# The 32 sample rows as four concurrent fp32 tiles, and the order of loads and products around two output blocks, in a decoder step on one core

## The reference

```python
def even_layer(...):                     # ends in
    out = concat([o_a, y]) @ W["w_out_even"][e]          # (rows, 512 + 1024) @ (1536, 1024)
def odd_layer(h, o_idx, W, past):
    proj = h @ W["w_in_odd"][o_idx]                      # h: rows x 1024
    q, k, v, glr, r = _split(proj, [512, 512, 1024, 16, 1024])
    lg = log_sigmoid(glr @ W["gla_w_gate2"][o_idx] + W["gla_b_gate"][o_idx]) / GLA_TAU
    ...
    return o @ W["w_out_odd"][o_idx], st                 # (rows, 1024) @ (1024, 1024)
def apply_layer(x, c, pos, l, W, past):
    shift, scale, gate = split(silu(c) @ W["w_mod"][l] + W["b_mod"][l])
    h = rms_norm(x, W["norm_w"][l]) * (1 + scale) + shift
    out, st = ...
    return x + gate * out, st
```

## Time and profile before

| | |
|---|---|
| median of three executions | 1732.21 us |
| the profiled execution | 1730.93 us, span 1729.3 us, mean granted clock 0.97 |
| TensorE busy | 1593.2 us, 92% of the span |
| weight loads / VectorE / ScalarE / GpSimd busy | 1273.3 / 794.7 / 611.5 / 379.5 us |
| DMA | 129.90 MB, mean 75 GB/s |
| even output block | 1003 to 1180 us |
| GLA projection | from 1180.5 us, value products to about 1299 us |
| odd output block | 1610 to 1729 us |

### The profile page before, as it was taken

The page is one execution under the profiler, slowest core; times in us unless marked ns, Lnnn a source line. Parts: engine busy times, 40 slices in busy tenths (PEclk is TensorE's granted clock), DMA queues, the critical chain, the costliest instruction groups (busy, mean ns, idle before and its releaser), DMA issues. The chain is left out here.

```text
span 1729.3 us, 27074 instructions
## 1 busy us (share of the span) xinstructions
PE 1593.2 (92%) x11401; PEld 1273.3 (74%) x11401; DVE 794.7 (46%) x1283; ACT 611.5 (35%) x1144; POOL 379.5 (22%) x244
## 2 busy tenths in 40 slices
PE   4899899999999899999999869998999999998698
PEld 4589676666666799999887648876999955554485
DVE  3443202666666676610588544224313344445443
ACT  4334211655555532321265433325322302222221
POOL 1142000101100132321598632111121200000231
PEclk9999999999999999999999979998999999997799
DMA  9322543421111011111011382102101120003621
GB/s 330 104 85 49 127 98 117 126 99 50 50 50 50 5 50 49 37 49 41 13 37 38 91 244 73 49 40 80 50 1 37 39 97 0 25 25 111 222 101 63
DMA packets 119678, 129.90 MB, mean 75 GB/s; under 512 B 16728, under 2 KB 91914, under 8 KB 119430
## 3 DMA queue, kind: packets, MB, share of 16 engines
q1 hardware_dynamic: 118950, 127.56, 23.6%
q0 software_dynamic: 608, 0.63, 0.3%
HBM read 107.05 MB, written 23.18 MB: 75 GB/s over the span
## 5 line engine op out<-in xcount | busy, mean ns | idle before, releaser
L154 PE MATMUL banks<-h_T_rest,w_ssd_high 128*128 128x352 f32 x480 | 156.3, 326 | 0.0
L154 PE MATMUL banks<-h_T_high,w_ssd_high 128*128 128x352 f32 x480 | 156.1, 325 | 0.0
L154 PE MATMUL banks<-h_T_high,w_ssd_rest 128*128 128x352 f32 x480 | 155.5, 324 | 0.0
L154 PE MATMUL banks<-w_r,h_T 128*128 128x512 f32 (+1 forms) x320 | 116.4, 551 | 0.0
L1403 DVE TENSOR_REDUCE pe_T<-banks 128x1 f32<-128x512 f32 (+7 forms) x108 | 81.9, 764 | 37.9 <-PE banks L154 37.3
L154 PE MATMUL banks<-out_even_w_high,mix_high 128*128 128x512 f32 (+1 forms) x216 | 86.7, 401 | 12.5 <-DVE out_even_w_rest L2334 12.5
L1320 ACT ACTIVATE p_att<-banks,pe_T 128x512 f32<-128x512 f32 (+7 forms) x128 | 86.2, 679 | 16.2 <-DVE pe_T L1403 15.3
L154 PEld LDWEIGHTS banks<-h_T_high,w_ssd_rest 128*128 128x128 f32 x480 | 91.1, 190 | 0.0
L154 PEld LDWEIGHTS banks<-h_T_high,w_ssd_high 128*128 128x128 f32 x480 | 90.3, 188 | 0.6 <-issue 0.6
L3048 DVE SCALAR_TENSOR_TENSOR gla_state<-gla_state,chunk_decay,banks 128x256 f32<-128x256 f32 x128 | 52.3, 475 | 83.5 <-PE banks L154 83.4
L154 PEld LDWEIGHTS banks<-w_r,h_T 128*128 128x128 f32 (+1 forms) x320 | 49.6, 175 | 55.4 <-issue 53.9
(11 more groups left out here) (499 smaller groups left out, 3701.5 us busy)
## 6 DMA issues: line engine op xcount, KB each, us to landing
w_mod_late<-in_w_mod_dram SPq DMA_DIRECT2D x8, 2048.0 KB, 8.1
w_ssd<-in_w_in_even_dram SPq DMA_DIRECT2D x20, 512.0 KB, 3.9
w_mod_rows<-in_w_mod_dram SPq DMA_DIRECT2D x4, 2048.0 KB, 20.7
xin<-in_x_prompt_dram SPq DMA_DIRECT2D x8, 512.0 KB, 11.3
cmp_w<-in_nsa_cmp_w_dram SPq DMA_DIRECT2D x8, 512.0 KB, 7.5
silu_z_T<-in_state_ssd_dram SPq DMA_DIRECT2D x8, 512.0 KB, 4.2
out_dram<-silu_z_T SPq DMA_DIRECT2D x8, 512.0 KB, 3.8
out_even_x_rows<-in_x_prompt_dram SPq DMA_DIRECT2D x8, 512.0 KB, 3.6
```

What stands on the lines that cost most here:

```text
L154: return nc.tensor.matmul(out, lhsT, rhs, start=start, stop=stop, skip_group_check=True)
```

## The change

Five edits. (1) In `block_out_rows` all weight loads are issued first; the gate, bias, x tiles, sample gates and `w_glr` or `final_w` come after. (2) The samples become tile 4 of the order (`OUT_TILES`). Their product is fp32 without a split, k mod 4 choosing the partition group, the moving operand first the high part of the weights and then their rest; ScalarE and VectorE copy the four partial sums to `out_parts`, and `sample_fold` adds them with two fp32 matmuls in the middle of tile 5. (3) The low-rank products of the first two chunks move from the GLA block to the output block, between the last tile's products and its turn; the third stays. (4) The first half of the value weights is loaded in the output block, once the last but one tile is done, and ScalarE and VectorE handle them first in the GLA block. (5) The samples' value products become fp32 in four groups, from a copy of the samples' h that GpSimd makes; the fold now contracts 128 rows. Buffers move with this (`mix_parts`, `out_parts`, `h_s`).

```diff
+SAMPLES_TURN = 4
+OUT_TILES = [m for m in range(NTP)]
+OUT_TILES.insert(SAMPLES_TURN, NTP)
...
+def low_rank_products(e, h2, c, bank):
...
+    s, n = CHUNKS[c]
+    for k in range(KD):
+        j = k % 4
+        last = mm(e.nc, e.ps[32 * j:32 * (j + 1), bank, 0:n], e.w_glr[:, k, :], h2[:, k, s:s + n], k < 4, k >= 4)
+    return last
...
                         sp.dma_start(w[:, k, :], W[k * P:(k + 1) * P, :]).then_inc(w_in[k], 16)
-                    if k == 1:
-                        sp.dma_start(gate[:, :], e.gate_save[l, 0].partition_broadcast(P)).then_inc(gate_in, 16)
...
-                    if 3 <= k < 6:
-                        load_x(k - 3)
...
+                sp.dma_start(gate[:, :], e.gate_save[l, 0].partition_broadcast(P)).then_inc(gate_in, 16)
+                sp.dma_start(y[:, 1, :], e.b_mod[l, 2 * D:3 * D].partition_broadcast(P)).then_inc(gate_in, 16)
+                for i in range(3):
+                    load_x(i)
+                for b in range(DB):
+                    sp.dma_start(gate_s[b * DS:(b + 1) * DS, :], e.gate_save[l, 1 + b].partition_broadcast(DS)).then_inc(gate_s_in, 16)
+                if final_w is not None:
+                    sp.dma_start(final_w[:, :], e.final_norm_w.partition_broadcast(P)).then_inc(final_in, 16)
+                else:
+                    sp.wait_ge(glr_zeroed, 1)
+                    sp.dma_start(e.w_glr[:, :, 0:16], e.w_in_odd[0, :, O_GLR:O_R].rearrange("(k p) n -> p k n", p=P)).then_inc(glr_in, 16)
...
+                        if n == NT - 2:
+                            sp.wait_ge(done, NT - 1)
+                            load_w_v(sp, e, 0)
...
+                def sample_products(n):
+
+                    for half in range(2):
+                        cols = slice(half * 512, (half + 1) * 512)
+                        for k0 in range(0, K, 4):
+                            for i, w_part in enumerate((whi, wlo)):
+                                for j in range(4):
+                                    k = k0 + j
+                                    last = mm(nc, e.ps[32 * j:32 * (j + 1), 2 * (n % 2) + half, :], mix(k, k + 1)[:, 0, TP:T], w_part[:, k, cols].bitcast(F32),
+                                              k0 == 0 and i == 0, k0 + 4 == K and i == 1)
+                    last.then_inc(parts_done, 1)
+
+                def sample_fold(n):
+
+                    pe.wait_ge(parts_act, 1)
+                    pe.wait_ge(parts_dve, 1)
+                    for half in range(2):
+                        last = mm(nc, e.ps[0:TS, 2 * (n % 2) + half, :], e.F["fold"], part[:, half * 512:(half + 1) * 512], True, True)
+                    last.then_inc(done, 1)
...
+                    if m == SAMPLES_TURN:
+                        sample_products(m)
+                        turn(m - 1)
+                        continue
                     for k in range(K):
                         if m == 2 and k == K // 2:
                             turn(0)
+                        if m == SAMPLES_TURN + 1 and k == K // 2:
+                            sample_fold(m - 1)
                         last = product(m, k)
                     last.then_inc(done, 1)
                     turn(m - 1)
+                if h2 is not None:
+                    pe.wait_ge(glr_in, 16)
+                    pe.wait_ge(scaled, NT - 1)
+                    pe.wait_ge(put_act, len([x for x in OUT_TILES[:EARLY] if x < NTP]))
+                    pe.wait_ge(put_dve, EARLY)
+                    for c in range(2):
+                        low_rank_products(e, h2, c, 2 + c)
                 turn(NT - 1)
...
-                for c, (s, n) in enumerate(CHUNKS):
-                    for k in range(KD):
-                        j = k % 4
-                        last = mm(nc, e.ps[32 * j:32 * (j + 1), 5 + c, 0:n], e.w_glr[:, k, :], h2[:, k, s:s + n], k < 4, k >= 4)
-                    last.then_inc(glr_done, 1)
+                low_rank_products(e, h2, 2, 7).then_inc(glr_done, 1)
...
+                def sample_rows(c, bank):
...
+                    for k0 in (0, 4):
+                        for x, w in enumerate((wv_hi, wv_lo)):
+                            for j in range(4):
+                                last = mm(nc, e.ps[32 * j:32 * (j + 1), bank, 0:256], h_s[:, k0 + j, :], w[:, c % 2, k0 + j, :].bitcast(F32), k0 == 0 and x == 0, k0 == 4 and x == 1)
+                    return last
...
                 for m in range(2):
+                    high_v(0, (m,))
                     high_h(m)
-                glr_copy(0)
+                for c in range(2):
+                    glr_copy(c)
...
+                nc.gpsimd.tensor_copy(h_s[:, :, :], h2[:, :, TP:T]).then_inc(h_kept, 1)
                 nc.gpsimd.memset(wg2[:, :], 0.0).then_inc(g_zeroed, 1)
...
-                    dve.wait_ge(glr_done, (m * P + rows(m) - 1) // (T // 3) + 1)
+                    if m * P + rows(m) > CHUNKS[2][0]:
+                        dve.wait_ge(glr_done, 1)
                     dve.wait_ge(h_high, m + 1)
+                    if m == NTP:
+                        dve.wait_ge(h_kept, 1)
...
-                rest_h(0)
-                rest_h(1)
                 for j in range(2):
                     dve.wait_ge(v_high, j + 1)
                     k = slice(4 * j, 4 * j + 4)
                     nc.vector.tensor_tensor(wv_lo[:, 0, k, :], wv[:, 0, k, :], wv_hi[:, 0, k, :].bitcast(F32), ALU.subtract).then_inc(v_rest_first, 1)
+                    rest_h(j)
```

More of the change, by code:

```diff
@@ L2158, in block_out_rows @@
         parts = [(0, by_head), (by_head, K)] if by_head else [(0, K)]
-        tok = lambda m: slice(m * P, m * P + rows(m))
+        size = lambda n: rows(OUT_TILES[n])
+        split = lambda n: len([m for m in OUT_TILES[:n + 1] if m < NTP])
+        tok = lambda n: slice(OUT_TILES[n] * P, OUT_TILES[n] * P + size(n))
         with nc.Block() as block:
@@ L2227, in turn @@
                         return
-                    r = rows(m)
+                    r = size(m)
                     pe.wait_ge(normed, m + 1)
                     if m >= 2:
-                        pe.wait_ge(put_act, min(m - 1, NTP))
+                        pe.wait_ge(put_act, len([x for x in OUT_TILES[:m - 1] if x < NTP]))
                         pe.wait_ge(put_dve, m - 1)
@@ L2265, in high @@
                     for a, b in parts:
-                        nc.scalar.copy(mhi[:, m % 2, a:b, 0:rows(m)], mix(a, b)[:, :, tok(m)]).then_inc(mix_high, 1)
+                        nc.scalar.copy(mhi[:, 1 - m % 2, a:b, 0:size(m)], mix(a, b)[:, :, tok(m)]).then_inc(mix_high, 1)
                 high(0)
@@ L2273, in _ @@
                 for m in range(NT):
-                    r, ym = rows(m), y[0:rows(m), m % 2, :]
-                    if m + 2 < NT:
+                    r, ym = size(m), y[0:size(m), m % 2, :]
+                    if m == SAMPLES_TURN:
+                        act.wait_ge(parts_done, 1)
+                        nc.scalar.copy(part[:, 0:512], e.ps[:, 2 * (m % 2), :]).then_inc(parts_act, 1)
+                    if m + 2 < NT and m + 2 != SAMPLES_TURN:
                         high(m + 2)
@@ L2311, in rest @@
                     for i, (a, b) in enumerate(parts):
-                        dve.wait_ge(mix_high, len(parts) * m + i + 1)
-                        nc.vector.tensor_tensor(mlo[:, m % 2, a:b, 0:rows(m)], mix(a, b)[:, :, tok(m)], mhi[:, m % 2, a:b, 0:rows(m)].bitcast(F32), ALU.subtract).then_inc(mix_rest, 1)
+                        dve.wait_ge(mix_high, len(parts) * (split(m) - 1) + i + 1)
+                        nc.vector.tensor_tensor(mlo[:, 1 - m % 2, a:b, 0:size(m)], mix(a, b)[:, :, tok(m)], mhi[:, 1 - m % 2, a:b, 0:size(m)].bitcast(F32), ALU.subtract).then_inc(mix_rest, 1)
                 def put(m):
@@ L2341, in _ @@
                 for m in range(NT):
-                    r, s = rows(m), ss[0:rows(m), m % 2:m % 2 + 1]
+                    r, s = size(m), ss[0:size(m), m % 2:m % 2 + 1]
+                    if m == SAMPLES_TURN:
+                        dve.wait_ge(parts_done, 1)
+                        nc.vector.tensor_copy(part[:, 512:1024], e.ps[:, 2 * (m % 2) + 1, :]).then_inc(parts_dve, 1)
                     dve.wait_ge(done, m + 1)
@@ L2476, in block_gla_proj @@
         sem = lambda s: new_sem(nc, "gla_" + s)
-        v_in, q_in = [[sem(f"w_v_in{i}{j}") for j in range(2)] for i in range(2)], [sem("w_qk_in0"), sem("w_qk_in1")]
+        v_in, q_in = e.w_v_in, [sem("w_qk_in0"), sem("w_qk_in1")]
         v_rest_first = sem("w_v_rest_first")
@@ L2549, in _ @@
                             pe.wait_ge((v_act, v_dve)[g % 2], g // 2 - 1)
+                        elif g >= 2:
+                            pe.wait_ge(glr_ready, g - 1)
                         out = e.ps[0:r, g % 4, 0:256]
-                        for k in range(KD):
+                        for k in range(KD) if m < NTP else ():
                             if g == 0 and k % 4 == 0:
@@ L2589, in v_copy @@
```

(7 more changed lines are left out.)

102 lines of the change are left out of this document (51 added, 51 removed).

## The result

The changed kernel takes 1714.41 us in the median of its four runs (1713.5 to 1716.06), the one before 1729.6 (1725.76 to 1733.26) beside it: ratio 0.9914, 95% interval 0.9886 to 0.9941. It is faster by 0.9%. The forecast was 1710, the range 1702 to 1719. The profiled execution took 1713.63 us (span 1712.0) against 1730.93 (span 1729.3): 17.3 us less, where the sum said 21.9.

A forecast was written before the change was run, and what follows sets the result against it. TensorE was taken to set the time. Terms 5.1 + 4.4 + 2.9 + 3.8 + 4.1 + 2.3 - 0.7 = 21.9 us off 1730.93 gave 1709.0, stated as 1710 because the runs' median lay 1.3 higher; range 1702 to 1719.

The forecast's parts named there:

- Starts (5.1 and 4.1): Starts of the even and odd output blocks: issuing weight loads first removes TensorE's stalls, gaining 5.1 and 4.1 us.
- The fear that the odd block's gate would hold VectorE: Odd block's start: gate and final weight, now last in the queue, hold VectorE; a wait reaches TensorE from 1637 on.
- Even and odd samples (4.4 and 2.3): Samples tile of both output blocks: fp32 passes, four running together, plus the fold; gain 4.4 us even, 2.3 odd.
- switches of the tile form: Around fp32 groups and folds: some 16 changes between 128- and 32-column tiles; 0 in the sum, 0 to 2.6 us in range.
- Value products (3.8): Samples tile of the GLA value products: 8 groups, 1.8 us instead of 2.75, four times; gain 3.8 us.
- Border (2.9): Even output block to GLA projection: first value product 4.3 us sooner, less 0.9 and 0.5; gain 2.9 us, bounds 1 and 4.
- the clock: At the border: clock possibly still at half for 12 to 24 value products; cost 0.9 us, within 0 to 2.4.
- Tail (+0.7): Behind the odd block's last matmul: store of 512 KB instead of 128 lands in 2.6 us instead of 1.9; cost 0.7.
- Late starts: Output block starts: weights come no sooner, or gate and final weight hold VectorE; 9.2 us gone, 1719; chance 0.12.
- Fall of the clock in the fp32 groups: Samples' fp32 groups: clock drops to half, groups take twice as long; +28 us instead of -10.5, 1748; chance 0.04.
- Four passes not together: Samples' fp32 groups: four passes don't run together at 512 columns; +63 us instead of -10.5, 1784; chance 0.02.
- Late fold or norm: Both output blocks: a slow VectorE split makes the fold or norm late; 2 us each, 1714; chance 0.08.

The follow-up runs named there:

- experiment 2: Changed kernel with the loads of both output blocks back in the old order: 1720.1 us.
- experiment 3: Kernel before with only the new order of the loads at both output blocks: 1717.65 us, ratio 0.992 to the kernel before.
- experiment 4: Changed kernel with all fp32 sample products of both output blocks on the first 32 partitions, so no two run together: 1764.72 us.
- the second profile: Changed kernel run and profiled again, no edit: 1713.66 us, ratio 0.9896 to the kernel before.
- experiment 6: Changed kernel with the first half of the value weights loaded at the GLA block's start again: 1712.58 us in one run.
- experiment 7: Changed kernel with all low-rank products back in the GLA block, value weights still early: 1711.38 us in one run.
- Experiment 10: Changed kernel plus unused matmuls in TensorE's idle times, with the last rows normed and stored in two column halves: 1708.11 us, ratio 0.9866 to the kernel before.

## Why the prediction was right, point by point

- **Starts (5.1 and 4.1): right**, 5.3 and 4.4 by the stretches. The order of the loads alone makes them (experiments 2, 3). One side figure was wrong and cost nothing: the gate and its kin landed at 1037.5, not before 1033; VectorE, done with both gates, still stood 4.85 us before the first tile came. The fear that the odd block's gate would hold VectorE didn't come true: TensorE's one idle time up to its first scaled tile is that for the first weights (8.37 us).
- **Even and odd samples (4.4 and 2.3): mechanism right, size 4.0 and 1.8.** 24 groups x 0.43 = 10.3 and 16 x 0.43 = 6.9 are as forecast, and so is the fold (four passes, 1.72). The missing step is "switches of the tile form", put at 0: the loss is 0.3 us around a group of fp32 matmuls, two groups to a block, 0.6 us. The bound there of 0 to 2.6 us for sixteen changes held it: four pairs in the output blocks and four in the value chunks, eight times 0.3, are 2.4.
- **Value products (3.8): 2.7.** The same 0.31 us per chunk, and groups of 1.72 instead of 1.8: 0.95 + 0.08 - 0.31 = 0.72, four times 2.9 where the stretch has 2.7. The fold's share of it I didn't separate.
- **Why the bound was not in the sum:** I read "no idle time is printed" in the earlier trace rows as "no cost". Those rows are changes of the columns within fp32r. The change to fp32 in a narrow tile was nowhere in the rows I used, though the trace of before has it around the groups in the scan (experiment 4), and such a loss isn't printed as idle; only starts minus pace show it.
- **Border (2.9): 1.8.** The first value product came as forecast (-4.2 against -4.3), the later start too (0.7 against 0.5). The step that was mis-sized is the clock: 0.9 us put, 1.7 measured (1.3 in the second profile), within its bounds of 0 to 2.4. I had taken a value between the two levels; the whole stretch of low-rank products and the first twenty value products ran at the lower one. And I credited the gain to two edits together. Experiments 6 and 7 part them: the value weights are worth 3.8 us at the first value product and some 5 over the border, moving the low-rank products none.
- **Tail (+0.7): +1.7.** The term took the landing time of stores in the middle of the block (2.6 against 1.9 us). What counts is the wait behind the last one, 1.5 us for 128 KB and 3.2 for 512, with the start of that wait unchanged. Experiment 10 speaks for the size as the cause: the second half, 256 KB, was waited for 1.7 us, less than either value of the whole. It is one profile, and why the whole took 3.2 us in seven and 2.2 in two is open.
- **The rivals.** Late starts: excluded by the stretches and by experiments 2 and 3. Fall of the clock in the fp32 groups: it stayed at 1.00. Four passes not together: experiment 4 is that case made real; it costs 31 + 21 us in the two output blocks. Late fold or norm: TensorE has no idle time in the even block between 1014.67 and the last turn, so neither the mix's rest at tile 6 nor the norm of tile 3 was late.
- **The sum.** 18.3 us by the touched stretches where 21.9 were forecast: 0.9 for samples in the output blocks, 1.1 for value products, 1.1 at the border, 1.0 at the tail, less 0.5 that the starts brought above their terms. The remaining 1.0 us to the profile's 17.3 is the net of the two untouched stretches, which move by several us from one execution to the next. What moves them there is only argued (the clock goes with it in the scan); ahead of the even block I haven't found the place.

## What to carry to other kernels

Look first at what the queue sends ahead of the data that an engine stands waiting for: reordering loads, with no change of work, was over half of this gain. Before paying for moving work into an idle hole, check what else ends at the same moment; here the weights did; the moved products were worth nothing with them and a loss without them, since TensorE then stood with its clock down. And price a change of tile width on TensorE by starts minus pace, since such losses aren't printed as idle.

## What the runs showed of the hardware

- A group of fp32 matmuls with 32 columns of weights cost 0.3 us around it (going in, coming out and at the next matmul), whether one column tile or four were in use and whether fp32r or fp32 stood beside it. fp32 with 128 columns between fp32r products cost nothing, and neither did fp32r with 32 columns beside fp32r with 128.
- Four fp32 passes of 512 columns on four column tiles took 0.43 us, one alone 0.43 too.
- Matmuls without use in the idle times kept the granted clock at 1.00 through the border, where it was 0.50 without them, and took 5.2 to 5.8 us off the touched stretches (5.2 between the medians, 1713.66 and 1708.46).
- 512 KB of weights loaded as two halves of 64 partitions landed every 2.34 us, as one load of 128 partitions every 1.28.
- Executions differ by up to 6 us in a stretch whose code is the same in every kernel (4.4 us between two of one kernel, 305.6 and 310.0), so one profile's span can't size an edit of 2 us; its own stretch can, to 0.1 us in the output blocks' tiles.
